# Spreading per-token numbers over the partitions with two fp32r products in place of one fp32 product

## The reference, cut to what matters

```python
def _rms(x, g):
    xf = x.astype(jnp.float32)
    y = xf * lax.rsqrt(jnp.mean(xf * xf, axis=-1, keepdims=True) + EPS)
    return (y * g.astype(jnp.float32)).astype(x.dtype)

def _layer(x, li, ...):
    xn = _rms(x, norm_mix_g)
    z = jnp.einsum('btd,dc->btc', xn, w_in)
    ...                       # mLSTM branch with gates per token and head,
    ...                       # two attention branches, gates, w_branch
    x = x + jnp.einsum('btd,de->bte', merged, w_out)
    xn = _rms(x, norm_ffn_g)
    gu = jnp.einsum('btd,df->btf', xn, w_gate_up)
    g, u = jnp.split(gu, 2, axis=-1)
    return x + jnp.einsum('btf,fd->btd', jax.nn.silu(g) * u, w_down)

def odd_layer(x, norm_g, w_in, conv_w, w_out):
    h = rmsnorm(x, norm_g)
    ...                       # 8 head slots: softmax over three dilated
    ...                       # groups together, divided by its sum per token
    return x + jnp.concatenate([y_c, y_d], axis=-1) @ w_out
```

## Time and profile before

| | |
|---|---|
| median of 3 runs | 3000.08 us (2999.51 to 3002.38) |
| the profiled execution | 2998.1 us, of which its span is 2996.3 us |
| PE busy | 2946.7 us (98% of the span) |
| POOL, DVE, ACT busy | 2003.0, 1494.9, 674.3 us |
| granted PE clock, mean | 0.999 of full speed |
| fp32 products that spread numbers over the partitions | 6 at L594, 8 at L687, 8 at L1141, 2 halves at L1241, 1 at L1243 |

### The profile page before, as it was taken

The page is one execution under the profiler, slowest core; times in us unless marked ns, Lnnn a source line. Parts: engine busy times, 40 slices in busy tenths (PEclk is TensorE's granted clock), DMA queues, the critical chain, the costliest instruction groups (busy, mean ns, idle before and its releaser), DMA issues.

```text
span 2996.3 us, 37845 instructions
## 1 busy us (share of the span) xinstructions
PE 2946.7 (98%) x13898; PEld 2404.8 (80%) x13898; DVE 1494.9 (50%) x2571; ACT 674.3 (23%) x1490; POOL 2003.0 (67%) x2041
## 2 busy tenths in 40 slices
PE   8999999999999999999999999999999999999998
PEld 6887777888888887777888888888888888888887
DVE  7778883633324788775543322565321231424542
ACT  3265354200001345345110000000111111221000
POOL 6775545777777767454777777887776556565775
PEclk9999999999999999999999999999999999999999
DMA  4322222333233322221423333233333223222322
GB/s 147 98 89 61 71 68 67 126 101 95 95 95 125 102 85 85 64 64 60 130 93 97 98 95 103 91 99 96 93 97 106 78 83 101 78 85 78 97 93 77
DMA packets 86922, 274.37 MB, mean 92 GB/s; under 512 B 10368, under 2 KB 11008, under 8 KB 86784
## 3 DMA queue, kind: packets, MB, share of 16 engines
q1 hardware_dynamic: 85248, 270.44, 28.8%
q10 hardware_dynamic: 1536, 2.10, 0.3%
HBM read 266.21 MB, written 4.19 MB: 90 GB/s over the span
## 4 chain that ended last, share of the span: by engine, by line
PE 91%; DVE 7%; ACT 1%; issue 1%; POOL 0%; DMA 0%; SPq 0%; POOLq 0%; DVEq 0%; ACTq 0%
PE PS L528 59%; PE PS L566 14%; PE PS L837 5%; PE PS L845 3%; PE PS L603 1%; PE PS L883 1%; PE PS L895 1%; PE PS L1134 1%; PE PS L924 1%; PE PS L617 1%; DVE SQ L1833 1%; PE PS L907 1%; DVE SMALLS L1798 0%; PE PS L1109 0%; PE PS L1121 0%
## 5 line engine op out<-in xcount | busy, mean ns | idle before, releaser
L493 POOL TENSOR_TENSOR WL<-RAW,WH 128x512 fp32r<-128x512 f32 (+2 forms) x536 | 799.1, 1491 | 9.8
L485 POOL TENSOR_TENSOR POOL_C<-POOL_C 128x1 f32<-128x1 f32 x536 | 126.7, 236 | 921.9 <-PE PS L528 519.0
L528 PE MATMUL PS<-XNH,WH 128*128 128x512 f32 (+1 forms) x1712 | 674.2, 394 | 1.5 <-DVE TMP L2396 1.3
L528 PE MATMUL PS<-XNL,WH 128*128 128x512 f32 (+1 forms) x1712 | 666.9, 390 | 0.0
L490 POOL TENSOR_TENSOR WL<-RAW,WH 128x512 fp32r<-128x512 f32 x418 | 576.2, 1378 | 34.9
L486 POOL TENSOR_SCALAR WH<-RAW 128x1024 fp32r<-128x1024 f32 (+3 forms) x536 | 530.3, 989 | 0.3 <-issue 0.2
L528 PE MATMUL PS<-XNH,WL 128*128 128x512 f32 (+1 forms) x1712 | 423.1, 389 | 0.0
L528 PEld LDWEIGHTS PS<-XNH,WH 128*128 128x128 f32 (+1 forms) x1712 | 320.8, 187 | 71.3 <-issue 5.1
L528 PEld LDWEIGHTS PS<-XNL,WH 128*128 128x128 f32 (+1 forms) x1712 | 320.8, 187 | 68.5 <-issue 2.2
L528 PEld LDWEIGHTS PS<-XNH,WL 128*128 128x128 f32 (+1 forms) x1712 | 320.5, 187 | 68.0 <-POOL WL L493 0.4
L566 PE MATMUL PS<-WH,XNH 128*128 128x512 f32 x704 | 279.3, 397 | 8.4 <-ACT TB L1249 6.6
(11 more groups left out here) (396 smaller groups left out, 4506.1 us busy)
## 6 DMA issues: line engine op xcount, KB each, us to landing
RAW<-w_oslot SPq DMA_DIRECT2D x56, 512.0 KB, 3.6
RAW<-w_L0ffn SPq DMA_DIRECT2D x44, 512.0 KB, 3.6
RAW<-w_L1ffn SPq DMA_DIRECT2D x44, 512.0 KB, 3.5
RAW<-w_od SPq DMA_DIRECT2D x32, 512.0 KB, 3.5
RAW<-w_L0G SPq DMA_DIRECT2D x24, 512.0 KB, 3.6
RAW<-w_L1G SPq DMA_DIRECT2D x24, 512.0 KB, 3.6
RAW<-w_epg SPq DMA_DIRECT2D x16, 512.0 KB, 3.4
RAW<-w_eug SPq DMA_DIRECT2D x16, 512.0 KB, 3.6
```

Source lines behind the costliest of these rows:

```text
L485: nc.gpsimd.tensor_tensor(POOL_C[:, 1:2], POOL_C[:, 0:1], POOL_C[:, 0:1], ALU.add)
L493: nc.gpsimd.tensor_tensor(WL[:, half, at_:w], RAW[:, slot, at_:w], WH[:, half, at_:w].bitcast(F32), ALU.subtract).then_inc(S("weights_spli ...
L528: mm = nc.tensor.matmul(bank, w[:, slot, k * cols:(k + 1) * cols], x[:, k0 + k, :], start=first and j == 0 and w is WH and x is hi, stop=l ...
```

## The change

The number is first split: its high part is the number rounded to fp32r, its low part the rest. Two diagonals are made, into a new fp32r tile `SPR` of 2x512 columns, and two fp32r products, the second added to the first in PSUM, spread both. `halve` is the split on DVE (two small instructions), `diagonals` makes both diagonals on DVE, `across` is the pair of products on PE. In the gate sums the split is made for all 16 numbers at once and ACT makes eight blocks in place of four. The small tiles are laid out anew for `SPR` and `TINYR`. The single-column products of `sum_tokens`, the transposes and all fp32 products of the branches stay as they are.

```diff
@@ tiles
+        SPR = sb(ctx, "SPR", [P, 2, T], F32R)
+        TINYR = sb(ctx, "TINYR", [P, 32], F32R)
...
+        UH, UL = TINYR[:, 0:16], TINYR[:, 16:32]
+        RTH, RTL = UH[:, 0:4], UL[:, 0:4]
+        OSH, OSL = RTH, RTL
@@ PE
+            def across(out_, high, low):
+
+                for x in (high, low):
+                    mm = nc.tensor.matmul(out_, ONES[:, :].bitcast(F32R), x, start=x is high,
+                                          stop=x is low)
+                return mm
+
             def spread_roots(v, bank):
 
                 claim(bank)
                 pe.wait_ge(S("diag_rooted"), v + 1)
-                nc.tensor.matmul(PS[bank][:, :], ONES[:, :], SQ[:, 0, :], start=True, stop=True
-                                 ).then_inc(S("rt_spread"), 1)
+                across(PS[bank][:, :], SPR[:, 0, :], SPR[:, 1, :]).then_inc(S("rt_spread"), 1)
@@ PE, spread_u
-                    pe.wait_ge(*L("diag_ready", 4 * n + 4))
-                    nc.tensor.matmul(PS[b][:, :], ONES[:, :], DG, start=True, stop=True
-                                     ).then_inc(L("ub_ready"), 1)
+                    pe.wait_ge(*L("diag_ready", 8 * n + 8))
+                    across(PS[b][:, :], SPR[:, 0, :], SPR[:, 1, :]).then_inc(L("ub_ready"), 1)
@@ PE, spread_sums
-                nc.tensor.matmul(PS[5][:, :], ONES[:, :], SQ[:, 0, :], start=True, stop=True
-                                 ).then_inc(S("o_spread"), 1)
+                across(PS[5][:, :], SPR[:, 0, :], SPR[:, 1, :]).then_inc(S("o_spread"), 1)
@@ PE, end of the program
                 pe.wait_ge(S("diag_rooted"), 7 + half)
-                nc.tensor.matmul(PS[3][:, cols], ONES[:, :], SQ[:, 0, cols], start=True, stop=True
-                                 ).then_inc(S("rt_spread"), 1)
-            nc.tensor.matmul(PS[2][:, :], ONES[:, :], SQ[:, 0, :], start=True, stop=True).then_inc(S("rt_spread"), 1)
+                across(PS[3][:, cols], SPR[:, 0, cols], SPR[:, 1, cols]).then_inc(S("rt_spread"), 1)
+            across(PS[2][:, :], SPR[:, 0, :], SPR[:, 1, :]).then_inc(S("rt_spread"), 1)
@@ ACT, diagonal(n)
                     for h in range(M_HEADS):
-                        run(DG[:, h * P:(h + 1) * P], IDENT[:, :], ACT.Copy, L("diag_ready"),
-                            scale=U[:, 4 * n + h:4 * n + h + 1])
+                        for e, of in enumerate((UH, UL)):
+                            run(SPR[:, e, h * P:(h + 1) * P], IDENT[:, :], ACT.Copy, L("diag_ready"),
+                                scale=of[:, 4 * n + h:4 * n + h + 1].bitcast(F32))
@@ DVE
+            def halve(of, high, low):
+
+                then(V.tensor_scalar(high, of, 1.0, 0.0, ALU.mult, ALU.add))
+                then(V.tensor_tensor(low, of, high.bitcast(F32), ALU.subtract))
+
+            def diagonals(high, low, n0, n):
+
+                for e, of in enumerate((high, low)):
+                    ins = V.tensor_tensor(heads(SPR[:, e, n0 * P:(n0 + n) * P], n),
+                                          IDENT[:, :].unsqueeze(1).to_broadcast([P, n, P]),
+                                          of[:, n0:n0 + n].bitcast(F32).unsqueeze(2).to_broadcast([P, n, P]), ALU.mult)
+                return ins
+
             def roots(v):
 
                 dve.wait_ge(S("tok_root"), v + 1)
                 then(V.reciprocal(RTOK, RTOK))
+                halve(RTOK, RTH, RTL)
...
-                V.tensor_tensor(heads(SQ[:, 0, :], NT), IDENT[:, :].unsqueeze(1).to_broadcast([P, NT, P]),
-                                RTOK.unsqueeze(2).to_broadcast([P, NT, P]), ALU.mult
-                                ).then_inc(S("diag_rooted"), 1)
+                diagonals(RTH, RTL, 0, NT).then_inc(S("diag_rooted"), 1)
@@ DVE, gate sums: U is split once
+                then(V.tensor_scalar(UH, U, 1.0, 0.0, ALU.mult, ALU.add))
+                V.tensor_tensor(UL, U, UH.bitcast(F32), ALU.subtract).then_inc(L("u_ready"), 1)
@@ DVE, total_sums
-                V.tensor_tensor(heads(SQ[:, 0, :], NT), IDENT[:, :].unsqueeze(1).to_broadcast([P, NT, P]),
-                                OSUM[:, 4:8].unsqueeze(2).to_broadcast([P, NT, P]), ALU.mult
-                                ).then_inc(S("o_diag"), 1)
+                halve(OSUM[:, 4:8], OSH, OSL)
+                diagonals(OSH, OSL, 0, NT).then_inc(S("o_diag"), 1)
```

More of the change, by code:

```diff
@@ L43 @@
     ckvq_raw=4, sk_raw=4, sv_ready=4, dq_raw=4, dk_raw=4, dv_ready=4, nab_ready=1, nab_exp=2,
-    ln_ready=1, lf_ready=1, bg_ready=1, bg_taken=1, diag_ready=16, u_ready=1, den_ready=4, ub_ready=4, ub_taken=4, darg_ready=1,
+    ln_ready=1, lf_ready=1, bg_ready=1, bg_taken=1, diag_ready=32, u_ready=1, den_ready=4, ub_ready=4, ub_taken=4, darg_ready=1,
     pex_ready=17, ms_ready=4, sw_ready=4, kt_ready=3, ktm_copied=3, vw_ready=12, cl_ready=3,
@@ L187, in build @@
         TMP = sb(ctx, "TMP", [P, 2, T])
+        SPR = sb(ctx, "SPR", [P, 2, T], F32R)
+        TINYR = sb(ctx, "TINYR", [P, 32], F32R)
         SQA = sb(ctx, "SQA", [P, T])
-        small = sb(ctx, "SMALLS", [P, 512])
+        small = sb(ctx, "SMALLS", [P, 488])
         def overlay(*tensors, skip=0):
@@ L311, in build @@
         GA, ET = SQ, TMP
-        WS, BS, INV = overlay(("WS", [P, 4, P]), ("BS", [P, 4, P]), ("INV", [P, 4, 16]), skip=99840)
+        WS, BS, INV = overlay(("WS", [P, 4, P]), ("BS", [P, 4, P]), ("INV", [P, 4, 16]), skip=96 * K)
         OYH, OYL, OQK = overlay(("OYH", [P, 16, T], F32R), ("OYL", [P, 16, T], F32R), ("OQK", [P, 2, 6, T]))
@@ L321, in build @@
         ODC, OZ = overlay(("ODC", [P, 2, T]), ("OZ", [P, 2, 6, P]), skip=64 * K)
-        (OACC,) = overlay(("OACC", [P, 2, T]), skip=98 * K + 128)
+        (OACC,) = overlay(("OACC", [P, 2, T]), skip=96 * K + 96)
         OGD = TMP
@@ L1714, in roots @@
                 then(V.reciprocal(RTOK, RTOK))
+                halve(RTOK, RTH, RTL)
                 if v == 6:
                     for half in range(2):
-                        V.tensor_tensor(heads(SQ[:, 0, 256 * half:256 * half + 256], 2),
-                                        IDENT[:, :].unsqueeze(1).to_broadcast([P, 2, P]),
-                                        RTOK[:, 2 * half:2 * half + 2].unsqueeze(2).to_broadcast([P, 2, P]), ALU.mult
-                                        ).then_inc(S("diag_rooted"), 1)
+                        diagonals(RTH, RTL, 2 * half, 2).then_inc(S("diag_rooted"), 1)
                     dve.wait_ge(S("rt_spread"), 8)
                     return
-                V.tensor_tensor(heads(SQ[:, 0, :], NT), IDENT[:, :].unsqueeze(1).to_broadcast([P, NT, P]),
-                                RTOK.unsqueeze(2).to_broadcast([P, NT, P]), ALU.mult
-                                ).then_inc(S("diag_rooted"), 1)
+                diagonals(RTH, RTL, 0, NT).then_inc(S("diag_rooted"), 1)
                 dve.wait_ge(S("rt_ready"), v + 1)
@@ L1937, in layer @@
                 V.memset(MPREV[:, 0:4], M_INIT)
-                V.tensor_tensor(U.rearrange("p (n c) -> p n c", n=NT), i_pre,
-                                B.rearrange("p (n c) -> p n c", n=NT), ALU.subtract).then_inc(L("u_ready"), 1)
+                then(V.tensor_tensor(U.rearrange("p (n c) -> p n c", n=NT), i_pre,
+                                     B.rearrange("p (n c) -> p n c", n=NT), ALU.subtract))
+                then(V.tensor_scalar(UH, U, 1.0, 0.0, ALU.mult, ALU.add))
+                V.tensor_tensor(UL, U, UH.bitcast(F32), ALU.subtract).then_inc(L("u_ready"), 1)
                 dve.wait_ge(*L("u_ready", 1))
```

## The result

| | kernel before | changed kernel |
|---|---|---|
| median of 8 runs | 2999.44 us (2998.15 to 3002.38) | 3009.02 us (3008.23 to 3014.27) |
| profiled execution: own time, span | 2998.1, 2996.3 | 3014.27, 3012.5 |
| ratio, 95% interval | | 1.0034 [1.0025, 1.0043] |

The change made the kernel slower by 9.6 us, 0.3%. The prediction had it 6.6 us faster, and its range ended at 2998.0. So 16.2 us have to be found.

The account below looks back on a forecast made before the run. The prediction took PE's stream to bound the kernel (91% of the span); -3.25 - 3.25 - 0.4 + 0.9 - 0.6 = -6.6 us gave a median of 2993.5 us, range 2990.5 to 2998.0.

Parts of the forecast that it names:

- Nothing else has a price: Rest of the kernel: stream of chunks, DMAs and POOL's splits are the same, so no cost was given.
- Term 1: Gate sums in `mv`: eight fp32 products become fp32r pairs, each saving 0.407 us, -3.25 us.
- Term 2: Odd slots: eight products become pairs, DVE's second diagonal stays covered, -3.25 us.
- Term 3: Norm 0: diagonals ready at about 29.4, covered by 1.7 us, one saving, -0.4 us.
- Term 4: Opening pairs of norms 1 to 5: PE waits for the second diagonal, each loses 0.18 us, +0.9 us.
- Term 5: End of the program: half diagonals and fp32r products from the last reciprocal on, -0.6 us.
- D: Opening pairs and end: more gained than summed, 2990.3 to 2992.1 us; chance 0.07.
- B: Opening pairs: POOL slows the second diagonal by 0.76 us five times, +3.8, 2997.3 us; chance 0.12.
- C: mLSTM branch: stages behind the gate sums take their gain, 3.25 us go, 2996.8 us; chance 0.10.
- E: Behind the opening pairs: PE's new waits lower its clock, 12 us per pair of five, 3005.5 us; chance 0.02.
- F: All spreading products: a pair takes as long as the fp32 one, 0.86 us, near 3003.3 us; chance 0.03.

Follow-up runs that it names:

- b1: Changed kernel with EPS_C and POOL_C put into spare columns of SMALLS (496 columns), stage tiles behind it 32 bytes lower: 2993.92 us, ratio 0.998.
- f2: b1 with norms and odd slots undone, so pairs of products in the gate sums alone: 2995.14 us, ratio 0.9986.
- f4: b1 with norms, gate sums and odd slots undone, so the fp32 product everywhere: 2998.49 us, ratio 0.9998.
- f3: b1 with norms and gate sums undone, so pairs of products in the odd slots alone: 2996.59 us, ratio 0.999.
- b4: b1 with the single fp32 product and single diagonal of before in norms 1 to 5: 2992.59 us, ratio 0.9974.
- a4: a2 with the single fp32 product and single diagonal of before in norms 1 to 5: 2996.85 us.
- a2: Changed kernel with SMALLS at 496 columns in place of 488, stage tiles behind it 32 bytes higher: 2999.31 us, ratio 1.0003.
- a1: Kernel before with SMALLS at 504 columns in place of 512, stage tiles behind it 32 bytes lower: 3017.75 us, ratio 1.0063.
- b2: Kernel before with SMALLS at 544 columns in place of 512, stage tiles behind it 128 bytes higher: 3013.54 us, ratio 1.0045.
- c2: Kernel before with an unused 32-column tile ahead of WH; WH, WL and the stage tiles 128 bytes higher: 3039.67 us, ratio 1.0136.
- c3: c2 with a second unused 32-column tile ahead of IDENT, behind WL: 3053.43 us, ratio 1.0183.
- c1: Kernel before with an unused 32-column tile ahead of X, every tile 128 bytes higher: 3000.15 us, ratio 1.0003.
- a3: Kernel before with SMALLS at 496 columns in place of 512, stage tiles behind it 64 bytes lower: 3015.81 us, ratio 1.0058.
- c4: b1 with the two diagonals of norms 0 to 5 signalled one by one, PE waiting for each: 2991.55 us, ratio 0.9975.

## Why the prediction was wrong

**The step that failed** is the one headed "Nothing else has a price", with its sentence "The stream of chunks, the DMAs and POOL's splits are the same." The stream of chunks is the same by its instructions, and not by its addresses. The diff shows the new sizes of the small tiles, and I gave the layout no price at all: no term, no bound and no rival. It is worth +15.1 us in the changed kernel (its median against b1's; 16.6 by the kernel before beside each), 12.2 of which stand in four pieces of the chain; the count times 6.67 ns gives 19.5 as the most that it could be, since products that wait for something else don't show it. The range excluded the result for the same reason.

**Why it could have been asked.** The trace of before shows PE and its loads busy for nearly all of the time on operands from two areas, and the diff moves one of the areas by 4,128 bytes. The only fp32r products of before at other distances are 42 of the 48 with 76-column weights, whose weight tiles do not start in steps of 256 bytes; their groups are at 390 to 392 ns, so the size was not to be had from them. But an unknown cost has to be bounded, and the bound is wide where 2,928 products could each change by nanoseconds.

**The terms that were priced**, by what the runs show:

- *Term 1, gate sums, -3.25.* Right: 0.45 us for the pair in the chain, 8 x 0.41 = -3.3; f2 against f4 -3.35.
- *Term 2, odd slots, -3.25.* Mechanism right: 0.46 us for the pair in the changed kernel, no idle time ahead. 8 x 0.40 = -3.2 by the trace, -3.24 between the traces of f3 and f4, -1.9 by their medians. The cover was thinner than I gave it: in the slot of the changed kernel shown above the two diagonals took 3.38 us from 2380.19, not 1.45 each, and were ready 2.15 us ahead of the product at 2385.72, not 3.3.
- *Term 3, norm 0, -0.4.* Right in size in b1, with less cover than I gave it. DVE's timeline there:
```profile
26.35 0.68 DVE L1721 TENSOR_SCALAR TINYR<-SMALLS 128x4 fp32r<-128x4 f32 x1
...
27.27 3.15 DVE L1727 TENSOR_TENSOR SPR<-IDENT,TINYR 128x512 fp32r<-128x512 f32 x2
...
31.15 0.63 PE L597 MATMUL PS<-SPR,ONES 128*128 128x512 f32 x2
```
  The diagonals were ready at 30.42, not 29.4, which leaves 0.7 us and not 1.7.
- *Term 4, opening pairs, +0.9.* Right in direction, low in size: +0.25 us per pair in the changed kernel, +0.28 in b1, so +1.3. The step that was short is the start of PE's product behind DVE's end. I took 0.05 us from the earlier trace rows; here it is 600.88 - (599.44 + 1.29) = 0.15. b4 gives back 1.3 against b1, a4 2.5 against a2, both by medians whose intervals are wider than that.
- *Term 5, the end, -0.6.* Right: 4.52 us against the 4.5 forecast. Before, PE started 2985.50 - 2985.35 = 0.15 us behind DVE there, not the 0.13 that the prediction says; that changes nothing.

Together b1 measures -7.0 us, with an interval of -9.0 to -3.3, where the sum has -6.6. The range's lower end of 2990.5 left out a bit of D, which reached 2990.3; the result lies on the other side. That the sum was right did not help, since it was a sum over the instructions that the diff touches.

**The rivals.** B (POOL slows the second diagonal) did not happen in the opening pairs: 1.29 us for both. C (the mLSTM stage absorbs the gain) is refuted by f2. E (the clock) had the right sign for a wrong reason: the new waits of the opening pairs brought no slow stretch behind them, and the piece behind norm 1 was longer by the same 3.52 us in a1, which has no such waits. The low clock in norm 0 was in the one profiled execution of the changed kernel and not in b1's. F is refuted by the 0.45 us.

**What stays open.** Why the distance matters. PE reads the moving operand and the next weights from the same partitions at the same time (in norm 1 of the changed kernel the load of the next weights and the product of XNH and WH both start at 603.24); that they collide in something which repeats every 256 bytes fits all runs, but no run shows what it is. Nor do the runs explain why +64 costs 2.25 ns a product and -64 as much as 32 does, or all of why b2, with the same 351.67 us per piece, is 4 to 6 us faster than a1. A part of that is norm 0's stretch at the lower clock: in a1's profiled execution, which is its median, the product that spreads the roots starts at 33.68, in b2's at 31.08.

## What to carry to other kernels

When a diff adds or resizes a buffer, write down the start address of every operand of the hot stream before and after, and ask for a change against the operand read beside it; here 32 bytes in a scratch tile cost more than the whole edit could gain. In a kernel whose TensorE is never idle, keep the moving tiles and the weight tiles at the same residue modulo 256 bytes, and when every product of a stage is one to three per cent longer behind a change to an allocation, look there before looking at waits. And measure an edit against a control at its own addresses (f4 here), or its result holds the layout's as well.

## What the runs showed of the hardware

- An fp32r product of 512 columns takes 226.7 ns of PE's time when the moving operand and the loaded one start in step modulo 256 bytes, 2.25 ns more at +64, 6.67 ns more (2.9%) at +32, -32 and -64, and 5.7 (c2, c3) to 6.65 ns (b2) more at +128. When all tiles move together (c1) nothing changes. It works as well with the roles exchanged: 389 to 395 ns in c3 with WL streaming and XNH loaded, and 391 ns at +64 against 396 at -64 with WL streaming and CKVH loaded (a3, a2). The Trainium skill, page "SBUF — State Buffer", section "A bandwidth-pool intuition that's wrong (but worth ruling out)", gives the weight load a second, independent read port; read that way, nothing should have changed, and c3 at +54.5 us shows that the two are not wholly independent. The same page's section "Operand start alignment" asks for a multiple of the element size and says that it speaks of legality, not of speed; all the addresses here meet it, and differ in time.
- The same two diagonals on DVE took 1.29 us in norm 1, where POOL was idle but for their last 0.13 us, and 3.15 us in norm 0 of b1, where POOL was busy for 5.83 of the 6 us around them.
- Splitting one product into two that wait for separate signals cost PE nothing visible between them: the opening pair of c4 is 0.29 us shorter than b1's.
